# Compressing the sample group's cached keys and values two sequences at a time

## What is computed

```python
def compress(x, pe, w1, w2):          # x: N, L, G=2 heads, hd=64;  32-token windows, stride 16
    m, nch = 2, L // 16
    ch = x[:, :nch * 16].reshape(N, nch, 16, G, hd)
    w1 = w1.reshape(m, 16, hd, 128)
    hsum = 0
    for r in range(m):
        proj = einsum('ncsgd,sdh->ncgh', ch + pe[r][:, None, :], w1[r])
        hsum = hsum + proj[:, r:r + nch - 1]
    return einsum('ncgh,hd->ncgd', gelu(hsum), w2)
```

## Time and profile before

| | |
|---|---|
| median of 3 runs | 1255.57 us (1252.93 to 1257.82) |
| profiled execution, its own time | 1253.22 us |
| its span, first to last instruction | 1251.5 us |
| PE busy | 1220.4 us (98%), 6878 matmul instructions |
| DVE, ACT, POOL busy | 667.9, 309.3, 255.4 us |
| L1330, the products, PE | 93.8 us, 768 instructions |
| page loads, L1061 | 128 DMAs of 128 KB |
| granted TensorE clock, mean | 0.999 |

### The profile page before, as it was taken

The page is one execution under the profiler, slowest core; times in us unless marked ns, Lnnn a source line. Parts: engine busy times, 40 slices in busy tenths (PEclk is TensorE's granted clock), DMA queues, the critical chain, the costliest instruction groups (busy, mean ns, idle before and its releaser), DMA issues.

```text
span 1251.5 us, 19571 instructions
## 1 busy us (share of the span) xinstructions
PE 1220.4 (98%) x6878; PEld 956.9 (76%) x6878; DVE 667.9 (53%) x1496; ACT 309.3 (25%) x696; POOL 255.4 (20%) x428
## 2 busy tenths in 40 slices
PE   7999999999999899999999999999999999999999
PEld 5787656877777667667788887788888888888887
DVE  6756364765565441141135715359777888863331
ACT  3422522544444312112000115221212121110000
POOL 4642002333432523223000200130101010100000
PEclk9999999999999999999999999999999999999999
DMA  6442474322334799897383111122222222302240
GB/s 229 172 152 72 145 269 175 94 86 70 104 100 146 224 327 353 273 344 266 128 346 115 71 68 34 37 79 72 84 85 85 84 78 87 140 25 93 93 159 18
DMA packets 83411, 174.58 MB, mean 139 GB/s; under 512 B 11153, under 2 KB 48850, under 8 KB 82418
## 3 DMA queue, kind: packets, MB, share of 16 engines
q1 hardware_dynamic: 65506, 115.40, 27.7%
q10 hardware_dynamic: 13648, 47.45, 10.1%
q0 software_dynamic: 4160, 10.49, 2.5%
HBM read 163.21 MB, written 10.09 MB: 138 GB/s over the span
## 4 chain that ended last, share of the span: by engine, by line
PE 90%; DVE 4%; ACT 2%; issue 2%; POOL 1%; DMA 1%; SPq 0%; ACTq 0%; DVEq 0%; POOLq 0%
PE ps L2789 20%; PE ps L2826 11%; PE ps L2568 10%; PE ps L1862 10%; PE ps L658 7%; PE ps L1330 5%; PE ps L2601 4%; PE ps L751 3%; PE ps L1263 2%; PE ps L1235 2%; PE ps L1249 2%; PE ps L2649 1%; PE ps L650 1%; PE ps L1962 1%; PE ps L736 1%
## 5 line engine op out<-in xcount | busy, mean ns | idle before, releaser
L2789 PE MATMUL ps<-arena 128*128 128x272 f32 x1120 | 257.1, 392 | 0.6 <-DVE arena L3128 0.6
L2789 PEld LDWEIGHTS ps<-arena 128*128 128x128 f32 x1120 | 212.7, 190 | 44.9 <-DVE arena L3128 1.1
L1862 PE MATMUL ps<-arena 128*128 128x272 f32 x512 | 121.8, 395 | 0.5 <-PE ps L1962 0.5
L2826 PE MATMUL ps<-arena 128*128 128x272 f32 x528 | 121.8, 392 | 0.0
L1862 PEld LDWEIGHTS ps<-arena 128*128 128x128 f32 x512 | 95.8, 190 | 26.8 <-issue 8.3
L2826 PEld LDWEIGHTS ps<-arena 128*128 128x128 f32 x528 | 100.3, 190 | 20.7
L1330 PEld LDWEIGHTS ps<-arena 128*128 128x128 f32 x768 | 88.2, 192 | 12.1 <-issue 11.2
L1330 PE MATMUL ps<-arena 128*128 128x128 f32 (+1 forms) x768 | 93.8, 279 | 2.0 <-DVE arena L1457 1.8
L658 PE MATMUL ps<-arena 128*128 128x272 f32 x392 | 91.7, 394 | 2.3 <-POOL arena L459 1.8
L658 PEld LDWEIGHTS ps<-arena 128*128 128x128 f32 x392 | 74.0, 190 | 19.3 <-POOL arena L459 2.2
L2568 PE MATMUL ps<-arena 128*128 128x272 f32 (+2 forms) x320 | 75.1, 393 | 0.0
(11 more groups left out here) (382 smaller groups left out, 1739.2 us busy)
## 6 DMA issues: line engine op xcount, KB each, us to landing
arena<-in_w_close SPq DMA_DIRECT2D x68, 512.0 KB, 3.4
arena<-in_pages_cmp SPq DMA_DIRECT2D x128, 128.0 KB, 2.1
arena<-in_past_va ACTq DMA_DIRECT2D x6, 2048.0 KB, 12.5
arena<-in_w_down SPq DMA_DIRECT2D x16, 704.0 KB, 5.9
arena<-in_past_ka ACTq DMA_DIRECT2D x6, 1792.0 KB, 10.6
arena<-in_w_close ACTq DMA_DIRECT2D x16, 512.0 KB, 6.8
arena<-in_w_proj SPq DMA_DIRECT2D x15, 512.0 KB, 3.3
arena<-in_pages_ks SPq DMA_DIRECT2D x96, 64.0 KB, 4.7
```

Source lines behind the costliest of these rows:

```text
L1862: last_one = pe.matmul(ps[:, gate_bank(q), 0:HALF], ring[:, n % CLOSE_RING, k * P:(k + 1) * P], m.h[:, k, half * HALF:(half + 1) * HALF], ...
L2789: last = pe.matmul(ps[:, bank(f, i), 0:HALF], w[:, k * P:(k + 1) * P], halved[:, rhs, k, :], start=(k == 0), stop=(k == 3))
L2826: last = pe.matmul(ps[:, down_bank(i, j), 0:HALF], w[:, k * P:(k + 1) * P], rhs[:, k, :], start=(k == 0), stop=(k == KH - 1))
```

## The change

Two sequences are compressed together, keys or values at a time: 8 pairs n instead of 16 halves. Each product has twice the columns (252 or 256) and there are half as many. They stand in three steps: EVEN in step 4 + 5n, ODD in 5 + 5n, accumulated on EVEN in the same PSUM slot, BOTH in 6 + 5n. Between EVEN and ODD ACT copies EVEN out (`take_even`), and POOL makes E(i) - E(i+1) of it (`slopes`). After BOTH, ACT takes E + O with the bias straight into the hidden tile (`take_first`), DVE makes the odd windows in two operations (`add`), and POOL's `bend`, ACT's tanh and DVE's `hidden` run once on 508 columns where they ran twice on 254. On POOL the sums of pair n + 1 now come after `bend` of pair n. The second projections of both sequences of a pair stand three and four steps after BOTH of the values.

A page is loaded in two halves (keys, values), each 64 KB: 32 DMAs before each pair. The 32 page numbers are read once for keys and values. The first 32 DMAs stand where the first 16 stood, ahead of the tile stores and of w1. `next_sum` moves to a place of its own, twice as large; two constants of the sample stage are loaded later because they lay there.

```diff
-    def first_step(s, kv):
-        return 4 + (2 * s + kv) * 5 // 2
+    PAIRS = [(q, kv) for q in range(NSEQ // 2) for kv in range(2)]
+    def step_of(n, product):
+        return 4 + 5 * n + product
+    def last_step(n):
+        return step_of(n, BOTH)
+    def small_step(s):
+        return last_step(2 * (s // 2) + 1) + 3 + s % 2
...
+        def pages_of(q):
+            found = []
+            for p4 in range(2 * NPAGE // 4):
+                at = 2 * q * NPAGE + 4 * p4
+                _, four = nc.values_load_multi_w_load_instructions(
...
+        def load_pages(n, found):
+            _, kv = PAIRS[n]
+            for c, page in enumerate(found):
+                sp.dma_start(pages[:, n % 2, c, :],
+                             d["pages_cmp"][ds(page, 1), :, P * kv:P * kv + P].rearrange("a p n -> p (a n)"))\
+                    .then_inc(page_in[n % 2], 16)
...
         sp.wait_ge(m.z_full, m.products_done)
-        load_pages(0)
+        found = pages_of(0)
+        load_pages(0, found)
         m.store_tiles(sp)
         sp.dma_start(w1, d["w_cmp1"]).then_inc(w_in, 16)
         m.store_values(sp)
-        load_pages(1)
+        load_pages(1, found)
         sp.wait_ge(m.stored, 16 * 7)
         sp.wait_ge(m.h_scaled, QT + 1)
-        m.load_constants(sp)
-        for s in range(2, NSEQ):
-            sp.wait_ge(proj_full, products(s - 2, 1))
-            load_pages(s)
+        for n in range(2, len(PAIRS)):
+            if n % 2 == 0:
+                found = pages_of(n // 2)
+            sp.wait_ge(proj_full, product_done(n - 2, BOTH))
+            load_pages(n, found)
...
-        sums(*HALVES[0])
         for kv in range(2):
             bend(p_hid[:, kv, :, 0:C], p_inner[:, kv, :, 0:C], kv + 1)
-        for n, (s, kv) in enumerate(HALVES):
-            if n + 1 < len(HALVES):
-                sums(*HALVES[n + 1])
-            bend(hid[:, s % 2, kv, :, 0:NCMP_S], inner[:, kv, :, 0:NCMP_S], 2 + n + 1)
+        sums(0)
+        for n, (q, kv) in enumerate(PAIRS):
+            slopes(n)
+            if n >= 1:
+                pool.wait_ge(hid_ready, 2 + n)
+            bend(hid[:, kv, :, 0:NCMP_S], inner[:, :, 0:NCMP_S], 2 + n + 1)
+            if n + 1 < len(PAIRS):
+                sums(n + 1)
+        pool.wait_ge(proj_full, product_done(len(PAIRS) - 1, BOTH))
...
+        def take_even(n):
+            act.wait_ge(proj_full, product_done(n, EVEN))
+            if n >= 1:
+                act.wait_ge(slope_ready, SLOPE0 + n)
+            act.copy(even[:, :, :], slot(EVEN)).then_inc(second_ready, 1)
+        def take_first(n):
+            q, kv = PAIRS[n]
+            act.wait_ge(proj_full, product_done(n, BOTH))
+            if q >= 1:
+                act.wait_ge(s_full, s_index["small", 2 * q - 1] + 1)
+            act.activation(windows(kv)[:, 0], slot(ODD), ACT.Identity, bias=m.cmp_bias[:, kv:kv + 1])\
+                .then_inc(second_ready, 1)
...
+            for s1 in range(8):
+                if product == BOTH:
+                    out = slot(BOTH).rearrange("p (e q) i -> p e q i", e=2)[:, :, :, 0:63]
+                    last = pe.matmul(out, w_both[:, kv, s1, :], follows[:, s1, :, :, 0:63], start=(s1 == 0), stop=(s1 == 7))
+                else:
+                    last = pe.matmul(slot(product), w1[:, kv, product, s1, :], x[:, product, s1],
+                                     start=(product == EVEN and s1 == 0), stop=(s1 == 7),
+                                     skip_group_check=(product == ODD))
+            last.then_inc(proj_full, 1)
...
         def small(s):
             b, n = s_slot(("small", s)), NCMP_S
-            pe.wait_ge(hid_ready, 2 + 2 * s + 2)
+            pe.wait_ge(hid_ready, 2 + 2 * (s // 2) + 2)
...
+            dve.wait_ge(second_ready, 2 + 2 * n + 2)
+            dve.wait_ge(slope_ready, SLOPE0 + n + 1)
+            step.done(dve.scalar_tensor_tensor(out=between, in0=slot(BOTH)[:, :, 0:63], scalar=m.cmp_bias[:, kv:kv + 1],
+                                               in1=slope[:, :, 0:63], op0=ALU.add, op1=ALU.add))
+            step.wait()
+            dve.tensor_tensor(between, between, slot(ODD)[:, :, 0:63], ALU.subtract).then_inc(proj_free, 1)
```

More of the change, by code:

```diff
@@ L933, in attend_prompt @@
     C = NCMP_P
[L935 removed]
+    pages, w1 = at(17016, 2, 2 * NPAGE, P), at(25208, 2, 2, 8, P)
     vc = at(29304, 2, P)
@@ L1004, in attend_prompt @@
             s_users.append(("cmp", 0))
-        s_users += [("small", s) for s in range(NSEQ) if seq_step(s) + 3 == t]
+        s_users += [("small", s) for s in range(NSEQ) if small_step(s) == t]
     s_index = {u: n for n, u in enumerate(s_users)}
@@ L1165, in prompt_small, with bend @@
             last.then_inc(s_act, 1)
[L1167 to L1176, removed]
+        def take_even(n):
+            act.wait_ge(proj_full, product_done(n, EVEN))
+            if n >= 1:
+                act.wait_ge(slope_ready, SLOPE0 + n)
[7 more added lines that the diff above has]
+                .then_inc(second_ready, 1)
+        def bend(n):
+            act.wait_ge(inner_ready, 2 + n + 1)
+            if n >= 1:
+                act.wait_ge(hid_ready, 2 + n)
+            act.activation(bent[:, :, 0:NCMP_S], inner[:, :, 0:NCMP_S], ACT.Tanh, scale=GELU_IN)\
                 .then_inc(bent_ready, 1)
@@ L1198, in steps @@
                 for s in range(NSEQ):
-                    if seq_step(s) + 3 == t:
+                    if small_step(s) == t:
                         small(s)
[L1201 to L1207, removed]
+                for n in range(len(PAIRS)):
+                    if step_of(n, EVEN) == t:
+                        take_even(n)
+                    if last_step(n) == t:
+                        take_first(n)
                 if 0 <= t - 2 < U:
                     take_turned(t - 2)
+                for n in range(len(PAIRS)):
+                    if last_step(n) + 1 == t:
+                        bend(n)
                 if t == C_TURN:
@@ L1355, in steps @@
                 for s in range(NSEQ):
-                    if seq_step(s) + 3 == t:
+                    if small_step(s) == t:
                         small(s)
[L1358 to L1364, removed]
+                for n in range(len(PAIRS)):
+                    for product in (EVEN, ODD, BOTH):
+                        if step_of(n, product) == t:
+                            piece(n, product)
                 if t in fills:
@@ L1525, in on_dve @@
         for t in range(STEPS + 4):
[L1526 to L1529, removed]
+            for n in range(len(PAIRS)):
+                if last_step(n) + 1 == t:
+                    add(n)
             if t == P_PROJ + 1:
@@ L1543, in on_dve @@
                 prompt_hidden()
[L1544 to L1547, removed]
+            for n in range(len(PAIRS)):
+                if last_step(n) + 2 == t:
+                    hidden(n)
             if t == C_SCORES:
```

138 lines of the change are left out of this document (68 added, 70 removed).

## The result

The changed kernel takes 1303.42 us (median of 4 runs, 1301.43 to 1306.41) against 1256.69 us of the kernel before (4 runs, 1252.93 to 1259.11): a ratio of 1.0373, 95% interval 1.0352 to 1.0393. The forecast was 1288 and the range ended at 1302: slower as forecast, and 1.4 us beyond the range.

What follows compares the result with a forecast made beforehand. PE's stream, busy 98% of the span, was taken to set the time. The terms summed as 1253.2 - 3.4 + 5.6 + 1.6 + 2.2 + 28.4 = 1287.6, say 1288 us; range 1255 to 1302.

Steps and rivals of the forecast that it cites:

- Products, -3.4: PE's product stream: half as many instructions of 256 or 252 columns, 84.8 us in place of 88.2, 3.4 gained.
- w1, +5.6: Start: w1, queued behind SP's extra page readings and issues, lands at 208.5; PE wants it at 202.84 and stands 5.6 us.
- The clock behind it, +1.6: After PE's stand for w1, a stretch at 1.2 GHz as in the earlier trace: 1.6 us lost, range 0 to 2.
- The prompt's second projection, +2.2: POOL's doubled first sums fall on DVE's scaling in steps 3 and 4, delaying the prompt's `hidden` by about 2.2 us.
- Light steps, +28.4 net of waits: Steps without products: POOL's sums block DVE's scaling, so PE waits 33.3 us over seven pairs, less 4.9 of old waits.
- the worked example, pair 4: Steps 26 to 28: scaling waits for the last of `bend`, then for the first sums operation; PE waits 6.1 us.
- the chain without blocking: Lower bound in steps without products: DVE's and ACT's chains alone give 2.5 us of PE waits, so 2.4 us gained.
- the old layout: Kernel before: two steps in three said to hold products, and never two in a row without.
- The clock in the light steps: Steps without products: clock drops counted only in the upper bound of 38 us, as three drops.
- Nothing for the pages and the late constants: Pages land ahead of their pair and the two moved constants are wanted late: no cost.
- The 13 us of work that DVE and ACT were to save: `add`, `take_even`, `take_first`, `bend` and `hidden` shrink DVE's and ACT's work by some 13 us, beside PE, counted at nothing.
- Rival (a): No blocking in the steps without products, which then cost what they save: 1256 us, chance 0.22.

Runs made afterwards that it cites:

- w1 early: Changed kernel with half of the first pages loaded ahead of the tile stores and w1, the other half behind them: 1285.55 us, ratio 1.0236 to the kernel before.
- the steps spread: Changed kernel with w1 ahead of half of the first pages, sums behind the slopes, and BOTH one step later (7 + 5n): 1252.07 us, ratio 0.9972.
- the kernel without sums: Changed kernel with w1 ahead of half of the first pages and POOL's sums of pairs 1 to 7 left out but for one element: 1263.9 us.
- the moved sums: Changed kernel with POOL's sums of pair n behind the slopes of pair n, no longer behind the bend of pair n - 1: 1280.92 us, ratio 1.0181.
- both edits: Changed kernel with w1 ahead of half of the first pages and POOL's sums behind the slopes: 1265.58 us, ratio 1.0078.

## Why the prediction was wrong in size

- **Products, -3.4: right.** 3.56 and 3.50 us a group at full clock, forecast 3.55 and 3.50. The four-element runs cost nothing at 252 columns.
- **w1, +5.6: right.** It landed at 208.2 (forecast 208.5), and PE stood 5.80 us. Counting SP's queue gave the landing to 0.3 us.
- **The clock behind it, +1.6: this step failed.** It took the length of a low stretch from the earlier trace rows as if it belonged to the stand. There wide work followed at once; here the compression's narrow instructions followed. The late w1 costs 17.9 us by the run that undoes it (w1 early), so 12.1 stand where 1.6 stood: this term was 10 us too small, and its range was 0 to 2.
- **The prompt's second projection, +2.2: about right in size, at another place.** The small projection did not wait. The first sums held up the transposes instead: by 2.09 us in the steps spread, at full clock, a wait that is gone when these sums move. In the changed kernel PE waited 1.43 us there, with the clock low just before. The w1 run still has these sums where they were, so its 12.1 us hold little of this term; in the sum below, what there is of it falls to the last one.
- **Light steps, +28.4 net of waits: mechanism right, waits too large.** PE's idle time from 235 to 440 us is 24.8 us against a forecast of 33.3. By pair, forecast and measured: 0: 4.3, 2.7. 1: 0.8 + 5.4, 0.9 + 2.8. 2: 1.2, 3.9. 3: 6.5 + 1.9, 5.4 + 0.5. 4: 6.1, 2.6. 5: 2.5 + 4.6, 1.8 + 2.0. 6: 0, 0.5. The places were right but for pair 2. In the worked example, pair 4, both scaling operations went in around the end of `bend` and took 2.11 us, so the sums came too late to block them; that wait of 2.6 us stands unchanged in the kernel without sums. I gave 2.5 us in all to the chain without blocking; the kernel without the sums waits 13.3 us between 220 and 440 us, the tail included. So the blocking was made too large and the chain too small. The prediction also miscounts the old layout: `first_step` puts products in four steps of five, not in two of three; now it is three of five. No term used that count.
- **The clock in the light steps: this step failed too. It was in no term of the sum**, only in the upper bound, with three falls of 1.6. The mean of 0.91 over 205 us is 37 us at the lower level; the stretch behind the one wait at 344 us has 10.4 of them, where the earlier trace rows, the source of the 1.6, had 3.2. By difference, 48.4 + 3.4 - 5.8 - 12.1 - (24.8 - 4.9) = 14.0 us of the slowdown are left for it. This is an inference and not a run, and it is good to some 2 us, since the 12.1 is a difference of medians. It agrees with the moved sums giving back 22.5 us of time for some 14 us of waits.
- **Nothing for the pages and the late constants: right** as far as seen. Half pages landed in 1.9 us, and PE waited for no page. The 13 us of work that DVE and ACT were to save did not show: ACT's busy time fell by 3.6 us and DVE's, without its scaling operations, by 2.1. How much of DVE's saving is hidden by other operations that waited for POOL was not measured.

The terms make 1253.2 - 3.4 + 5.8 + 12.1 + 19.9 + 14.0 = 1301.6, the profiled execution's own time, but only because the last one is what was left over. The forecast came as near as it did by luck in part: it had the light steps' waits 8.5 us too large, and that hid a third of the 24.5 us of clock that it lacked. Rival (a) had its condition judged the right way and its price too low: with w1 early and no sums the time is 1263.9, where its logic without the late w1 would have given under 1250.

## What to carry to other kernels

Work that fills PE's steps is also what covers the other engines' chain: halving the number of pieces can cost more at the holes than it gains in the stream, and where the holes lie (one line here, 13.5 us) decided the sign: 0.8% above the kernel before with two light steps in a row, 0.3% below it without. A long operation on POOL that blocks DVE belongs beside PE's long work, not in its gaps (22.5 us here). A stand of PE must be priced with what runs behind it: 5.8 us of waiting were 17.9 us of time.

## What the runs showed of the hardware

- DVE's scaling waited for whole POOL operations of double length (5.51 us for 0.7 us of work), one operation slipping in between two of POOL's. This is the exclusive port pair that the Trainium skill describes (SBUF — State Buffer, "SBUF: two separate sides"), and the traces agree.
- After a stand of 5.80 us PE's clock stayed at 1.2 GHz for 24 us of nearly unbroken work, the 66-column compression and the steps behind it; with 16 instructions of 256 columns put first it was back at 2.4 GHz before the compression, which then took 7.26 us in place of 13.89. A stand of 2.03 us at this place was already followed by the low level; waits of 1.87 us before the transposes were followed by it in some executions (0.52 from 215 to 217 us with both edits) and not in others (1.00 in the steps spread).
